# Token-stationary projections taken two weight tiles at a time in a two-block transformer kernel

## The reference

```python
def hybrid_mixer(h, w_in, ...):
    z, xbc, dt_raw, q, k, v = split_sizes(h @ w_in, IN_SIZES)   # 1024, 2048, 16, 1024, 1024, 1024 columns
    xbc = silu(causal_dwconv(xbc, conv_w, conv_b))              # xs, bs, cs
    dt = softplus(dt_raw + dt_bias)
    y = ssd_scan(xh, dt, a, bs, cs) + d_skip * xh               # chunks of 128 tokens
    y = rms_norm_by_group(y * silu(z))
    o = rms_norm(diff_attention(q, k, v, lam, rel_bias))        # 8 heads, two softmaxes each
    return concatenate([y, o]) @ w_out

def nsa_mixer(h, w_in, ...):
    q, kc, vc, ks, vs, kw, vw, gates = jnp.split(h @ w_in, splits, axis=-1)   # 1024, then 6 x 256, then 48
    # compressed, selected and window branches; each has a softmax over its keys and its own values
    return (g0 * o_cmp + g1 * o_slc + g2 * o_win) @ w_o
```

## Time and profile before

| | |
|---|---|
| median of 3 runs | 1852.58 us (1851.62 to 1852.61) |
| profiled execution, time | 1850.84 us |
| profiled execution, span | 1849.0 us |
| PE busy | 1828.9 us, 99% of the span |
| DVE busy | 1304.1 us, 71% |
| ACT busy | 979.4 us, 53% |
| chain that ended last | PE 91%, DVE 6%, ACT 1% |
| granted TensorE clock, mean | 0.998 |
| first mixer, projections to last output tile | 197.6 to 431.4 us of the span |
| sparse attention, projections and loop | 1396.5 to 1525 us |

### The profile page before, as it was taken

How to read it: one execution, slowest core, us unless ns; L and a number is a source line. 1 busy time by engine, 2 the same in 40 slices (tenths; PEclk the granted TensorE clock), 3 DMA queues, 4 the chain that set the end, 5 groups by cost and what they waited for, 6 DMA issues and landing times.

```text
span 1849.0 us, 28458 instructions
## 1 busy us (share of the span) xinstructions
PE 1828.9 (99%) x11524; PEld 1619.8 (88%) x11524; DVE 1304.1 (71%) x1510; ACT 979.4 (53%) x1338; POOL 168.2 (9%) x190
## 2 busy tenths in 40 slices
PE   9999999999999999999999999999999999999998
PEld 7888999999898888888889888888889969898886
DVE  7875688777567765886685777567758787567763
ACT  6654465565455544554455555455544576455542
POOL 1200000133010001200120100000000004010000
PEclk9999999999999999999999999999999999999999
DMA  7555444434444554555444455555554505535553
GB/s 289 214 205 175 168 171 160 149 138 169 150 160 182 191 197 162 217 191 184 170 172 158 168 197 182 188 185 196 182 189 175 198 16 183 182 115 204 189 198 114
DMA packets 45720, 325.07 MB, mean 176 GB/s; under 512 B 5293, under 2 KB 5429, under 8 KB 6560
## 3 DMA queue, kind: packets, MB, share of 16 engines
q1 hardware_dynamic: 44208, 316.56, 47.5%
q0 software_dynamic: 1248, 6.77, 1.1%
q10 hardware_dynamic: 144, 0.00, 0.0%
HBM read 322.26 MB, written 1.06 MB: 175 GB/s over the span
## 4 chain that ended last, share of the span: by engine, by line
PE 91%; DVE 6%; ACT 1%; issue 1%; POOL 0%; DMA 0%; POOLq 0%; DVEq 0%; SPq 0%; ACTq 0%
PE PS L715 26%; PE PS L777 13%; PE PS L720 13%; PE PS L782 6%; PE PS L586 5%; PE PS L587 5%; PE PS L588 5%; PE PS L815 4%; PE PS L820 2%; DVE w_lo L2124 2%; PE PS L837 1%; PE PS L839 1%; PE PS L838 1%; PE PS L862 1%; PE PS L880 1%; DVE xT L2147 1%
## 5 line engine op out<-in xcount | busy, mean ns | idle before, releaser
L2124 DVE TENSOR_TENSOR w_lo<-raw,w_hi 128x2048 fp32r<-128x2048 f32 x295 | 681.1, 2313 | 250.0 <-ACT w_hi L1448 249.9
L715 PE MATMUL PS<-xT,w_hi 128*128 128x512 f32 x2096 | 660.0, 396 | 3.0 <-DVE arena L2296 2.5
L1448 ACT ACTIVATE w_hi<-raw 128x2048 fp32r<-128x2048 f32 x295 | 562.9, 1911 | 135.4 <-PE PS L588 88.5
L720 PEld LDWEIGHTS PS<-xT,w_lo 128*128 128x128 f32 x2096 | 393.7, 188 | 93.0
L720 PE MATMUL PS<-xT,w_lo 128*128 128x256 f32 x2096 | 411.8, 278 | 0.0
L715 PEld LDWEIGHTS PS<-xT,w_hi 128*128 128x128 f32 x2096 | 319.5, 189 | 3.8 <-DVE arena L2296 2.7
L777 PE MATMUL PS<-more_hidden,w_hi 128*128 128x512 f32 x480 | 150.8, 395 | 0.0
L1550 ACT ACTIVATE arena<-PS 128x512 f32<-128x512 f32 x66 | 39.4, 597 | 162.7 <-PE PS L720 162.7
L777 PE MATMUL PS<-mT,w_hi 128*128 128x512 f32 x384 | 120.6, 395 | 0.0
L586 PE MATMUL PS<-xT,w_hi 128*128 128x256 f32 x400 | 114.3, 286 | 0.3 <-DVE w_lo L2124 0.3
L587 PE MATMUL PS<-xT,w_hi 128*128 128x256 f32 x400 | 113.2, 283 | 0.0
(11 more groups left out here) (360 smaller groups left out, 3240.5 us busy)
## 6 DMA issues: line engine op xcount, KB each, us to landing
raw<-weights SPq DMA_DIRECT2D x299, 1024.0 KB, 4.8
arena<-mems POOLq DMA_DIRECT2D x5, 1024.0 KB, 6.0
x<-x_in SPq DMA_DIRECT2D x1, 1024.0 KB, 7.2
out<-x SPq DMA_DIRECT2D x4, 256.0 KB, 2.9
both<-toep POOLq DMA_DIRECT2D x1, 512.0 KB, 4.0
arena<-toep POOLq DMA_DIRECT2D x1, 512.0 KB, 4.7
con<-consts SPq DMA_DIRECT2D x1, 498.0 KB, 13.4
arena<-dtw SPq DMA_DIRECT2D x1, 256.0 KB, 13.3
```

The lines of the kernel that those rows point to most:

```text
L715: pe.matmul(PS[:, bank + part, :], w_hi[:, slot, w:w + P], xT[:, k].rearrange("p a b -> p (a b)"), start=k == 0, stop=False, skip_group_ch ...
L720: last = pe.matmul(PS[:, bank + part, 0:S], w_lo[:, slot, w:w + P], xT_hi[:, k, :], start=False, stop=k == KC - 1, skip_group_check=True)
L1448: act.activation(w_hi[:, slot, :], raw[:, raw_slot, :], ACT.Copy).then_inc(hi_ready, 1)
L2124: dve.tensor_tensor(w_lo[:, slot, :], raw[:, raw_slot, :], w_hi[:, slot, :], ALU.subtract).then_inc(lo_ready, 1)
```

## The change

- A new PE function `next_values` does two token-stationary tiles at once, as `value_tiles` does: for each half of the tokens 24 matmuls of 512 moving columns, 256 from each of two slots. It waits for both high parts first, does the 16 products with them, then waits for both low parts and does the 8 others. Work that stood between two tiles can be put between its halves (`mid`). Both tiles are released together at its end (`tile_used` by 2), and each half fills one bank.
- It is used for z1 z0, z2 z3, v0 v1 and v3 v2 of the mixer and for vw vs of sparse attention, so 480 matmuls of 256 columns become 240 of 512.
- `M_ORDER` becomes x0 x1 (z1 z0) x2 x3 (z2 z3) x4 q0 x5 k0 x6 q1 x7 (v0 v1) k1 q2 k2 q3 k3 (v3 v2); the places of splits and evacuations on ACT and DVE follow.
- `gate_z` and `value` on ACT do two activations of 512 columns for a pair (`evacuate_values`) in place of two of 256 for a tile.
- In sparse attention DVE's split of the tile after next moves from before the units' loop into it (at i = 4), and ACT's into i = 1, behind the values and ahead of unit 0's copy.

```diff
-M_ORDER = ["x0", "z0", "x1", "z1", "x2", "z2", "x3", "z3", "x4", "q0", "x5", "k0", "x6", "v0", "x7", "q1",
-           "k1", "v1", "q2", "k2", "v2", "q3", "k3", "v3"]
-N_ORDER = ["kc", "vc", "q0", "q1", "wk0", "wk1", "q2", "q3", "wv0", "wv1", "ks", "kw", "vs", "vw"]
+M_ORDER = ["x0", "x1", "z1", "z0", "x2", "x3", "z2", "z3", "x4", "q0", "x5", "k0", "x6", "q1", "x7", "v0",
+           "v1", "k1", "q2", "k2", "q3", "k3", "v3", "v2"]
+N_ORDER = ["kc", "vc", "q0", "q1", "wk0", "wk1", "q2", "q3", "wv0", "wv1", "ks", "kw", "vw", "vs"]
...
+            def next_values(mid=None):
+
+                n, b = at.tile, at.proj % 4
+                slots = slice(n % SPL, n % SPL + 2) if n % SPL < SPL - 1 else slice(0, SPL, SPL - 1)
+                pe.wait_ge(hi_ready, n + 2)
+                for m in range(TT):
+                    if at.proj + m >= 4:
+                        pe.wait_ge(bank_free[(b + m) % 4], (at.proj + m) // 4)
+                    o, t = PS[:, 4 + (b + m) % 4, :], slice(m * P, (m + 1) * P)
+                    for k in range(KC):
+                        f = slice(k * 256, (k + 1) * 256)
+                        pe.matmul(o, xT_hi[:, k, t], w_hi[:, slots, f], start=k == 0, stop=False, skip_group_check=True)
+                        pe.matmul(o, xT_lo[:, k, t], w_hi[:, slots, f], start=False, stop=False, skip_group_check=True)
+                    pe.wait_ge(lo_ready, n + 2)
+                    for k in range(KC):
+                        f = slice(k * 256, (k + 1) * 256)
+                        last = pe.matmul(o, xT_hi[:, k, t], w_lo[:, slots, f], start=False, stop=k == KC - 1,
+                                         skip_group_check=True)
+                    if mid is not None and m == 0:
+                        mid()
+                last.then_inc(tile_used, 2)
+                at.tile += 2
+                at.proj += 2
+
...
-                    taken(f"v{h // 2}")
+                    for j in (0, 1) if h < 4 else (2, 3):
+                        taken(f"v{j}")
...
-                next_proj("x", True, None, statistic_row)
+                next_proj("x", False, None, statistic_row)
...
+                next_values(decay_columns)
+                triu, ones = con[:, K_TRIU:K_TRIU + P], con[:, K_ONES:K_ONES + P]
                 turn_xs(0)
-                next_proj("x", True)
-                triu, ones = con[:, K_TRIU:K_TRIU + P], con[:, K_ONES:K_ONES + P]
                 next_proj("x", False)
                 pe.wait_ge(la_ready, 1)
...
                 turn_xs(1)
-                next_proj("x", True)
                 next_proj("x", False)
-                turn_xs(2)
-                next_proj("x", True)
+                next_values(lambda: turn_xs(2))
...
+                next_values(begin_scan)
                 for g in range(4):
-                    last = pe.matmul(PS[:, 2 + g // 2, (g % 2) * 256:(g % 2 + 1) * 256], btok[:, g, :], xdte[:, g, :],
-                                     start=True, stop=True, skip_group_check=True)
-                last.then_inc(prev_done, 1)
-                pe.wait_ge(xs_taken, 4)
-                pe.wait_ge(n_masks, 2)
-                segment(0)
...
+                def between_values():
+                    turn_o(0, 3)
+                    turn_probs(2, 2)
+                    logits(3, 0)
+                    weigh(1, 3)
+                    taken("q3")
+                    turn_y(0, 4)
+                    taken("k3")
+                    turn_y(1, 5)
+
+                next_values(between_values)
                 turn_o(1, 3)
-                taken("k3")
+                taken("v3")
                 turn_probs(3, 6)
                 pe.wait_ge(y_lo, 4)
                 logits(4, 4)
-                taken("v3")
...
+                def first_logits():
+                    turn_compressed()
+                    taken("kw")
+                    pe.wait_ge(cmp_ready, 4)
+                    pe.wait_ge(n_masks, 3)
+                    logits(0)
+                    logits(1)
+
+                next_values(first_logits)
...
+            def evacuate_values(outs, func=ACT.Copy, split_next=True, ahead=0):
+
+                act.wait_ge(rcol_ready, at.stat)
+                act.wait_ge(tile_used, at.tile + (2 if split_next else 2 - ahead))
+                if split_next:
+                    next_split()
+                for m in range(TT):
+                    v = PS[:, 4 + at.proj % 4, :]
+                    if len(outs[m].shape) == 3:
+                        v = v.rearrange("p (a b) -> p a b", a=2)
+                    act.activation(outs[m], v, func, scale=rcol[:, m:m + 1]).then_inc(bank_free[at.proj % 4], 1)
+                    at.proj += 1
+                if split_next:
+                    next_split()
...
                 act.wait_ge(lc_ready, 1)
                 act.activation(to_end, to_end, ACT.Exp)
                 act.activation(from_start, lc[:, 16:32], ACT.Exp).then_inc(decay_ready, 1)
+                first_tap(3)
+                evacuated()
                 convolved(2)
-                gate_z(2)
-                first_tap(3)
-                evacuated()
                 convolved(3)
-                gate_z(3)
+                gate_z(1)
                 first_tap(4)
                 evacuated()
...
                 decay(1)
-                evacuated()
+                next_split()
                 decay(2)
                 decay(3)
+                value(0, 1)
+                next_split()
                 y_squares(0)
                 y_scale(0)
-                value(1)
+                evacuated()
                 decay(4)
                 decay(5)
                 y_squares(1)
...
                 y_high(1, 5)
+                value(1)
                 o_high(1, 3)
-                value(3)
+                next_split()
                 turned_probs(3, 6)
                 o_squares(2, 7)
+                next_split()
                 exponential(4)
...
                     if i == 1:
-                        evacuate(vw, split_next=False)
+                        v = arena[:, A_VS:A_VS + 1024].rearrange("p (a b) -> p a b", a=2)
+                        evacuate_values([v[:, :, m * 256:(m + 1) * 256] for m in range(TT)], split_next=False)
+                        next_split()
...
                 dve.tensor_tensor(to_end, PS[:, 3, 64:80], lc[:, 0:16], ALU.subtract).then_inc(lc_ready, 1)
+                next_split()
                 take_xs(1)
                 taps(2)
-                next_split()
-                evacuated()
                 conv_input(3)
+                next_split()
+                taps(3)
                 take_xs(2)
-                taps(3)
-                next_split()
+                evacuated()
                 evacuated()
...
                 o_low(1, 3)
+                evacuated()
                 biased(4, 4)
-                evacuated()
                 combine(4)
+                evacuated()
                 o_low(2, 7)
...
                 maximum(0)
                 maximum(1)
-                evacuated()
                 probability(0)
                 probability(1)
                 for i in range(2, n + 3):
+                    if i == 4:
+                        evacuated()
                     if i < n:
```

More of the change, by code:

```diff
@@ L1195, in mixer @@
                 weigh(0, 3)
-                next_proj("x", False)
-                turn_o(0, 3)
-                turn_probs(2, 2)
-                logits(3, 0)
-                weigh(1, 3)
-                taken("v2")
-                turn_y(0, 4)
-                taken("q3")
-                turn_y(1, 5)
-                next_proj("x", True)
+                def between_values():
[8 more added lines that the diff above has]
+                next_values(between_values)
                 turn_o(1, 3)
-                taken("k3")
+                taken("v3")
                 turn_probs(3, 6)
@@ L1210, in mixer @@
                 logits(4, 4)
-                taken("v3")
+                taken("v2")
                 weigh(2, 7)
@@ L1331, in nsa, with turn_compressed @@
                 last.then_inc(cmp_done, 1)
[L1332 to L1340 removed]
+                def turn_compressed():
+                    pe.wait_ge(cmp_prob, 1)
+                    taken("ks")
+                    b = 4 + (p0 + names.index("ks")) % 4
+                    for t in range(TT):
+                        for u in range(2):
+                            last = pe.transpose(PS[:, b, (2 * t + u) * P:(2 * t + u + 1) * P],
+                                                pc[:, t, u * P:(u + 1) * P], ident)
+                    last.then_inc(cmp_turned, 1)
                 s, wT = area(A_S3, 2, 4, S), area(A_WT3, 4, 4, P)
@@ L1381, in weigh @@
                         taken("vw")
+                        taken("vs")
                     if t == 0 and c >= 2:
@@ L1782, in gate_z, with value @@
                 def gate_z(j):
-                    evacuate(z[:, :, j * 256:(j + 1) * 256], ACT.Silu)
-                def value(j):
```

(16 more changed lines are left out.)

86 lines of the change are left out of this document (35 added, 51 removed).

## The result

The changed kernel takes **1866.47 us** (median of 4, 1865.65 to 1868.15) against 1852.10 for the kernel before in the same comparison (median of 4, 1850.59 to 1852.61). The ratio is 1.0082, 95% interval 1.0070 to 1.0094: 0.82% slower, some 15 us. The forecast was 1861.9, slower by 9.3. The direction was right, the size too small by a third. The median lies at the very end of the range (1866.5); by the ratio (1852.58 x 1.0082 = 1867.8) the time is beyond it.

What follows compares the result with a forecast made beforehand. The prediction took PE to bound the kernel nearly everywhere. Its seven terms, -3.0 - 1.0 + 5.2 + 1.1 + 0.65 + 3.7 + 2.6, summed to +9.3 us, so 1861.9 us, with a range of 1853.5 to 1866.5.

Steps and rivals of the forecast that it cites:

- Term 1: The five pairs' own gain from 512-column matmuls on PE: 0.6 us a pair, -3.0 us in all.
- Term 2: PE's wait for the silu of `convolved(1)` ahead of `turn_xs(1)` goes: -1.0 us.
- Term 3: In the middle of pair z2 z3, PE waits for `convolved(2)` from about 243.5 to 248.7 us: +5.2 us.
- the rival that named it: The clock falls in PE's wait, slowing the pair's second half: 2.5 us more, 1864.4 us; chance 0.12.
- Term 4: The scan's group 2: DVE has one more evacuation and one more low split in its period, +1.1 us.
- term 5: Head 1's probabilities: DVE evacuates q3 ahead of `combine(1)`, delaying PE's `turn_probs(1)` by 0.65 us.
- Term 6: Behind pair v3 v2: `weigh(3)` comes 28.0 us after the pair's start (T), with about 0.4 coming back: +3.7 us.
- Term 7: Sparse attention: DVE's split delays unit 3's probability by 1.9 us, ACT's costs 0.4 at unit 0's copy: +2.6 us.
- the waits are as I sum them: Main case for the whole kernel: the sum as worked out, +9.3 us, 1861.9 us; chance 0.60.

Runs made afterwards that it cites:

- e5: Changed kernel with DVE taking x3's bank (`conv_input(3)`) ahead of `take_xs(1)` and `taps(2)`, not behind them: 1861.76 us, ratio 1.0051.
- e2: Changed kernel with 24 added matmuls of 512 columns, results never read, keeping PE busy in the wait inside pair z2 z3: 1865.53 us, ratio 1.0076.
- e7: Changed kernel with DVE evacuating q3 behind `combine(1)` instead of ahead of it: 1867.31 us, one execution.
- e3: Changed kernel with DVE's split behind sparse attention's loop instead of at i = 4: 1865.48 us, ratio 1.0076.
- e11: The changed kernel profiled once more, nothing altered: 1867.91 us.
- e10: The kernel before profiled once more, nothing altered: 1852.15 us.
- e8: Changed kernel, all five pairs kept, with the edits of e1 (`turn_xs(2)` behind pair z2 z3), e5, e6, e7, e3 and ACT's sparse-attention split moved: 1854.21 us, ratio 1.0014.
- e9: Kernel before with the two z pairs alone, `turn_xs(2)` behind the pair and x3's bank taken early: 1848.64 us, ratio 0.9984.
- e4: Changed kernel with both engines doing the last heads' work ahead of the splits behind the mixer's last pair: 1862.71 us, ratio 1.0059.
- e6: Changed kernel with e4's order, `o_low(2)` ahead of DVE's second low split and ACT's second high split behind `o_high(2)`: 1863.69 us, ratio 1.0064.

## Why the prediction was wrong in size

- **Term 1, right.** A pair's pitch is 0.228 us in the rows above, for 0.227, and in the mixer the single pairs' marks moved by 0.6 to 0.8. In sparse attention only 0.2 to 0.3 arrived.
- **Term 2, right.** The old wait is gone, -1.8 at `turn_xs(1)` for -1.6.
- **Term 3, the wait right, its consequence missing.** 5.75 us for 5.2, from 243.3 to 249.1 for 243.5 to 248.7, and the rows have the chain's links in the order that was walked; e5 takes two of them out and gains what they cost. The step that failed is the sum's clock term, put at nothing. The range's upper end took up no more than 0.4 us of it (1866.5 instead of 1866.1), and the rival that named it (2.5 us, which is what e2 measured) got 0.12. The argument against it was the 2.5 us gap of the earlier trace rows, which cost no clock in the one profile there was. That was one outcome of an event that goes the other way eleven times in thirteen.
- **Term 4 and term 5, right** (1.1 and 0.7). For term 4 the 1.1 was the middle between 0.3 and 1.9 and no reading of a row, so that it fits is luck in part. What e7 adds: in this place without slack on DVE, exchanging neighbours only moved the loss.
- **Term 6, size near, by two errors that cancel; return and clock wrong.** `weigh(3)` came 28.7 us after the pair's start (364.29) for 28.0. The middle of the pair was put 1.0 too long: the 1.04 us of the x8 row are both `turn_y` together, not one. So `turn_probs(4)` came at T + 26.0, where the sum has 26.7. From there to `weigh(3)` the sum has 1.34 us, and it took 2.7, since `weigh(3)` waits for `o_low(2)` (L2567), which stands on DVE behind a second low split (L2177) that the sum left out:

```profile
390.16 2.28 DVE L2177 TENSOR_TENSOR w_lo<-raw,w_hi 128x2048 fp32r<-128x2048 f32 x1
392.37 0.48 DVE L2567 SCALAR_TENSOR_TENSOR hT<-PS,small,hT 128x256 fp32r<-128x256 f32 x1
```

  Behind it I had 0.4 coming back. Instead 1.7 more were lost, with the clock at half: the waits of 1.25 and 0.71 us follow each other within 2.5 us, and the clock fell behind them. So a single long wait isn't needed. This was the largest miss beside term 3, and no rival had it. The 1.7 is a difference of marks: no run took the half clock away here and left the waits.
- **Term 7, right in its sum** (2.5 for 2.6), not in its parts: PE's wait for DVE ahead of unit 3's `turn_probs` is 1.3 us for 1.9 (e3 gains 1.5), and the one for ACT at unit 1 is 0.8 for an estimate of 0.4.
- **The gap near 750 us.** 2.0 of the 17.4 us between the two profiled executions (0.5 of a longer gap, the rest the clock) are no effect of the change: e11, the same program, has a gap of 2.5 us there, and e10 has the fall without the change. The first profile of before was a lucky one, and that it "lay 1.7 below the median" was a sign of it: one such fall costs 1.6. e10 and e11, both with the fall, differ by 15.8 us, and the medians by 14.4.

The sum without the clock is +9.3. With 2.5 for the first fall, 1.7 for the second, 0.4 for the return that did not come, and the excess of two rows (0.8 in term 3's row of the table, of which the wait is 0.55, and 0.7 in term 6's) it is 15.4, and 17.4 less the 2.0 of the gap is 15.4 too; the small misses of the other rows nearly cancel. So the chances were wrong at one place: "the waits are as I sum them" and "the clock falls behind them" are not rivals: behind the wait of 5.8 us the second came with the first in all six profiles.

## What to carry to other kernels

On a kernel in which PE hardly ever waits, price a new wait of PE by its length and by the half clock that follows. Here 5.8 us of idle time cost 2.5 us more, and behind short waits close together 1.7 went with the clock at half. A pair of tiles saves per matmul (0.6 us) but releases its slots together, so both splits come due at once on engines that had them spread: take it where those engines have slack before the next hand-over (the z tiles), and leave it where they follow PE by half a microsecond (heads, scan, sparse attention). That is how e8 and e9 read together; no run tried one of the other three pairs alone. Moving work in the order need not remove a wait: in e4, e6 and e7 the wait moved on, and the run gained less than its length or nothing. And before a difference of 2 us is explained, look at more than one profile of each kernel: a fall of the clock in unchanged code came and went.

## What was not expected of the hardware

- The clock's fall is not a fixed function of the gap. Behind the same 2.5 us gap in the same program it stayed at 1.00 once and fell to 0.50 once. Behind 1.9 us (e5) it stayed; in the wait of 5.8 us it fell in all six profiles that have it.
- Once fallen it stayed so while PE was fully busy, until about 254 us behind the long wait. There the price was 2.5 us in the changed kernel and 2.0 in e7, where the clock fell 1.1 us earlier in the same wait and was back as much earlier.
- Behind the gap near 750 us it was at half for about half as long in ten of the eleven profiles, and that cost 1.3 to 1.6 us; in e5 it lasted as long as behind the long wait and cost 2.8. In e10 it fell only 1.1 us after PE had gone on.
- What stays open: whether 2.5 us is worse in one place than another. No run here changed the code of the gap near 750 us.
